# A third tile pair of the cross-attention output product as seven half-size products

## Chip, cores and metric

One core of one Trainium2 chip runs the kernel as one program. The metric is the device time of an execution in microseconds (us). Everything is float32 unless a line says otherwise.

## The reference, cut to what matters

The kernel computes one layer of a bidirectional encoder for 768 tokens (256 of a prompt, 512 of a sample) of width 1024: a mixer (self attention and convolution), a cross attention into 256 memory tokens per sequence, and a mixture of experts. Each of the three is added to 2^0.25 times its input and normalised by a LayerNorm. The change lies in the last line of the cross attention and the LayerNorm behind it:

```python
p = jax.nn.softmax(sc, axis=-1).astype(v.dtype)
o = jnp.einsum('bhqk,bkhd->bqhd', p, v).reshape(b, s, D_MODEL)
return o @ w_o                                      # 768x1024 @ 1024x1024
...
h = _layer_norm(DEEPNORM_ALPHA * h + xa, ln2_g[l], ln2_b[l])
ff = _hier_moe(h, w_router_g[l], ...)               # logits = h @ router, top-1 group, top-2 experts
```

## The kernel before, in words

The 768 rows are six tiles (0 to 5) of 128 rows; `hres` holds them by rows, `hT` and `cat` hold transposed copies. Each engine has one program of its own, in a fixed order written by hand, and semaphores join them. PSUM's eight banks are handed out ahead of time by `plan_banks` (turns of four banks for products, two for transposes); a `claim` waits until the bank's last user has read it, `full` waits until a bank is filled.

**The output product.** The weight w_o lies in two slabs of 1024x512. For a pair of tiles (a = 0: tiles 0 and 1, a = 1: tiles 2 and 3), the pair is seen as a 2x2 block matrix (A11, A12, A21, A22: two tiles by two halves of the inner dimension), the weight as 2x2 blocks too, and the product is made from seven half-size block products P1 to P7 instead of eight (`co_term`, L2340 to L2345, matmuls on L2344). VectorE makes the sums of blocks that go into them: `row_sums` (L1682 to L1688, into `scr`) for the rows, and once the sums of the weights (L1397, L1725, L1726). It then adds each product into `hres` (`term_sum`, L1692 to L1707, L1506), except that ScalarE copies P1 out first (L1206). Tiles 4 and 5 are done plainly: for each tile and each half of the columns, eight matmul steps of 512 columns (`product`, L2008), which one VectorE instruction adds to the row (`residual`, L1461).

**The LayerNorm behind it (LN_2).** For tiles 0 to 4: VectorE takes mean and variance (`dve_stats`, L744 and L746), GpSimd makes two coefficients (`pool_coef`, L718 to L720), ScalarE scales the row (`act_hat`, L736), GpSimd multiplies by the gain (`pool_gain`, L729), VectorE adds the bias (`dve_bias`, L761) and signals `ln_done`. The list `SHORT` (L537) names norms that take a shorter way, tile 5 among them: after the statistics VectorE itself does (row - mean) x gain (L754), waits for GpSimd's coefficient, and does x rstd + bias (L757). ScalarE and GpSimd's gain are left out.

**Behind the norm, on TensorE:** `h2_T(i)` transposes tile i once `ln_done` has come (L2020), ScalarE copies it to `cat` (`rows_T`, L1002), and `route(i)` multiplies it by the 36 columns of the router (L2334). The order before is: pair 0's seven products; pair 1's with h2_T(0) ahead of P4; h2_T(1); the products of tile 4 with route(0) between its halves; h2_T(2); tile 5's with route(1); h2_T(3); route(2); h2_T(4); route(3); route(4); h2_T(5); route(5). Then VectorE turns the logits into tables of rows (L1758 on), and the mixture of experts begins with GpSimd's gathers of rows from DRAM (L905).

**On the DMA queue of SyncE:** the normalised tiles are stored to `h2_rows` (L649), each after its `ln_done`. Before the store of tile 2, the queue waits for P3 of the last pair and then loads expert 0's down weights and expert 1's gate and up weights (L632, L627), over buffers that the seven products used. After the last store it waits for the last output product and loads more experts. In the expert stage weights stream all the time, each load waiting until its buffer has been used.

```python
            for i in range(NT):                                        # SyncE
                if i == 2:
                    full(sp, ("co7", CO_PAIRS - 1, TERMS[-1]))
                    load_d(0, 0)
                    load_gu(1, 1)
                sp.wait_ge(ln_done, dones(LN_2[i]))
                sp.dma_start(h2_dram[i * P:(i + 1) * P, :], hres[:, i, :]).then_inc(h2_stored, 16)
```

Of the kernel before, what the change touches and what calls it, by code (L numbers as in the profile page):

```python
# [25 lines left out]
P = 128  # L26
# [4 lines left out]
NT = T // P  # L31
# [72 lines left out]
MEAN_AT, VAR_AT = 9, 12  # L104
TERMS = ("P1", "P2", "P6", "P7", "P4", "P5", "P3")
CQ_CHUNKS = KC // 2
CO_PAIRS = 2
MIX_TERMS = [(a, term) for a in range(2) for term in TERMS[:2]] + [(a, term) for a in range(2) for term in TERMS[2:]]
CO_WEIGHTS_AT = {10: 0, 12: 1, 14: 2, 16: 3}
TH = T // 2  # L110
# [42 lines left out]
def plan_banks():  # L153

    place, used, turn = {}, [0] * 8, {}

    def take(kind, key):
        banks = {"mm": (0, 1, 2, 3), "tr": (4, 5), "pv": (6, 7), "first": (4, 5, 6, 7)}[kind]
        b = banks[turn.get(kind, 0) % len(banks)]
        turn[kind] = turn.get(kind, 0) + 1  # L160
        place[key] = (b, used[b])
        used[b] += 1

    for i in range(NT):
# [12 lines left out]
    for key in ("qT", "kT"):  # L177
        turn["tr"] += turn["tr"] % 2

    def qk(i):  # L180
        take("tr", ("qT", i))
        take("tr", ("kT", i))

    qk(0)
    qk(1)
    for k in range(STEPS + 3):
        if k < STEPS:
            take("mm", ("sS", 2 * k))
# [36 lines left out]
    for a in range(CO_PAIRS):  # L225
        for term in TERMS:
            take("mm", ("co7", a, term))
    for i in range(2 * CO_PAIRS, NT):
        for j in range(2):
            take("mm", ("co", i, j))  # L230
    for i in range(NT):
        for j in range(2):
            take("tr", ("hT", 2, i, j))
    take("pv", "route")
    for key in ("rank", "count", "counts", "order", "caps"):
        take("mm", key)
    take("tr", "firstD")
    for key in ("firstA", "firstB"):
        take("pv", key)
    for key in ("base", "list"):  # L240
        place[key] = (7, used[7])
        used[7] += 1
    return place, used


def encoder(nc, x, mem, w_slabs, lnp, ln_cols, rope_cos, rope_sin, q_gain, k_gain, cpar_dram, w_router, b_router,
# [7 lines left out]
    with ExitStack() as ctx:  # L254
# [69 lines left out]
        co3 = 3 - sum(co_at)  # L324
        coT = {"T3": ring[:, co3, 0:2048], "T2": ring[:, co3, 2048:4096], "T4": early[:, 4096:6144], "T1": early[:, 6144:8192]}
        coS = {f"S{n + 1}": scr[:, 4096 + 512 * n:4608 + 512 * n].rearrange("p (k t) -> p k t", k=4) for n in range(4)}
        coU = [memx[:, 1024 * a:1024 * a + 512] for a in range(CO_PAIRS)]
        coV = [memx[:, 1024 * a + 512:1024 * a + 1024] for a in range(CO_PAIRS)]

        def co_rows(a):  # L330

# [186 lines left out]
        slab_last = {"a": ("a", CC - 1, 1), "g": ("g", CC - 1, 1), "q": ("q", NT - 1), "kv": ("kv", NT - 1)}  # L518
        for j in range(2):
            slab_last |= {f"mix{j}": (("mx", 0, "P5"), ("mx", 1, "P3"))[j], f"ck{j}": ("ck", 4 * j + 3), f"cv{j}": ("cv", "P4", MT // 2 - 1),  # L520
                          f"cq{j}": ("cq", "P3", CQ_CHUNKS - 1), f"co{j}": ("co", NT - 1, j)}


        slab_last["cv1"] = ("cq", "P5", CQ_CHUNKS - 1)
# [11 lines left out]
        LN_2 = [LN_1[-1] + 1 + i for i in range(NT)]  # L536
        LN_3 = [LN_2[-1] + 1 + i for i in range(NT)]  # L537

        SHORT = (LN_2[-1], LN_3[-1])
        FOLD = LN_X + LN_M  # L540

        def hats(n):
# [13 lines left out]
        def _(sp):  # L556
# [86 lines left out]
            for i in range(NT):  # L643
# [3 lines left out]
                    load_gu(1, 1)  # L647
                sp.wait_ge(ln_done, dones(LN_2[i]))
                sp.dma_start(h2_dram[i * P:(i + 1) * P, :], hres[:, i, :]).then_inc(h2_stored, 16)  # L649
            full(sp, ("co", NT - 1, 1))  # L650
            load_d(1, 1)
            load_gu(3, 3)
            load_d(2, 2)
# [111 lines left out]
        def _(pool):  # L765
# [170 lines left out]
                                ALU.mult).then_inc(low_ready, 1)  # L936
            pool.wait_ge(h2_stored, 16 * NT)
            pool.wait_ge(tabs_done, 1)
            full(pool, ("co", NT - 1, 1))
            gather(0)  # L940
            gather(1)
            pool.wait_ge(tabs_done, 3)
# [46 lines left out]
        def _(act):  # L989
# [211 lines left out]
                bank = full(act, key)  # L1201
                a.activation(cq_out(0, 1, c), bank[:, 0:TH], ACT.Copy, scale=MHD ** -0.5).then_inc(free(key), 1)
            exps("x", CROSS, STEPS)
            for a2 in range(CO_PAIRS):
                bank = full(act, ("co7", a2, "P1"))
                a.activation(coU[a2], bank, ACT.Copy).then_inc(free(("co7", a2, "P1")), 1)  # L1206
            act_hat(act, LN_2[0])
            act_hat(act, LN_2[1])
            rows_T(2, 0)
            rows_T(2, 1)  # L1210
            act_hat(act, LN_2[2])
            act_hat(act, LN_2[3])
            rows_T(2, 2)
            act_hat(act, LN_2[4])
            for i in range(3, NT):
                rows_T(2, i)

            act.wait_ge(h2_stored, 16 * NT)
# [47 lines left out]
        def _(dve):  # L1266
# [411 lines left out]
            def row_sums(a, part):  # L1678

                (A11, A12), (A21, A22) = co_rows(a)  # L1680
                if part == 0:
                    v.tensor_tensor(coS["S1"], A21, A22, ALU.add).then_inc(co_combined, 1)  # L1682
                    dve.wait_ge(co_combined, 5 + 6 * a)
                    v.tensor_tensor(coS["S2"], coS["S1"], A11, ALU.subtract).then_inc(co_combined, 1)
                    return
                v.tensor_tensor(coS["S3"], A11, A21, ALU.subtract).then_inc(co_combined, 1)
                dve.wait_ge(co_combined, 6 + 6 * a)
                v.tensor_tensor(coS["S4"], A12, coS["S2"], ALU.subtract).then_inc(co_combined, 1)  # L1688

            def add_term(a, term, i, j):  # L1690
# [49 lines left out]
            term_sum(1, "P5")  # L1740
            dve_stats(dve, LN_2[2], link)
            term_sum(1, "P3")
            dve_stats(dve, LN_2[3], link)
            for k in range(2 * CO_PAIRS, NT):
                for j in range(2):
                    residual(("co", k, j), k, j).then_inc(free(("co", k, j)), 1)
                    if k == 4:
                        dve_bias(dve, LN_2[2 + j], link)
                    was_read(dve, ("co", k, j))
                dve_stats(dve, LN_2[k], link)  # L1750
                if k == 4:
                    dve_bias(dve, LN_2[4], link)
            dve_bias(dve, LN_2[-1], link)


# [232 lines left out]
        def _(pe):  # L1988
# [333 lines left out]
                for c in range(CQ_CHUNKS):  # L2322
                    was_read(pe, ("cq", term, c))
            attention("x", CROSS, len(SELF))
            wo = [slab("co0"), slab("co1")]
            for j in range(2):
                was_read(pe, ("xO", CROSS[-1][0], j))

# [22 lines left out]
            for a in range(CO_PAIRS):  # L2351
                (A11, A12), (A21, A22) = co_rows(a)
                co_term(a, "P1", A11, coB[0][0])
                co_term(a, "P2", A12, coB[1][0])
                pe.wait_ge(co_combined, 6 + 6 * a)
                co_term(a, "P6", coS["S2"], coT["T2"])
                pe.wait_ge(co_combined, 7 + 6 * a)
                co_term(a, "P7", coS["S3"], coT["T3"])
                if a == 0:
                    pe.wait_ge(co_combined, 9)  # L2360
                else:
                    h2_T(0)
                co_term(a, "P4", A22, coT["T4"])
                if a == 0:
                    pe.wait_ge(co_combined, 10)
                co_term(a, "P5", coS["S1"], coT["T1"])
                pe.wait_ge(co_combined, 8 + 6 * a)
                co_term(a, "P3", coS["S4"], coB[1][1])
            h2_T(1)
            for i in range(2 * CO_PAIRS, NT):  # L2370
                for j in range(2):
                    last = product(("co", i, j), lambda k: k, lambda k: hTv[:, k, i * P:(i + 1) * P],
                                   lambda k: wo[j][:, k, :])
                    done(("co", i, j), last)
                    if j == 0:
                        route(i - 4)
                h2_T(i - 2)
            route(2)
            h2_T(NT - 2)
            route(3)  # L2380
# [215 lines left out]
```

## Time and profile before

| | us |
|---|---|
| runs: median (lowest to highest), 3 runs | 1031.46 (1028.77 to 1032.88) |
| the profiled execution's own time | 1032.55 |
| its span, first to last instruction | 1030.8 |
| TensorE matmul busy in the span | 912.4 |
| VectorE / ScalarE / GpSimd busy | 528.8 / 237.0 / 316.4 |
| mean granted TensorE clock, as a share of 2.4 GHz | 0.952 |

Times in a profile count from the start of the span. A row of a timeline merges instructions of one kind that follow each other; "x16" counts records, and two records are one matmul step here. What stands in brackets behind a row is the idle time of the engine ahead of it and who ended it.

### The profile page before, as it was taken

What the parts mean: (1) busy time and instruction counts of PE and PEld (TensorE: products, weight loads), DVE (VectorE), ACT (ScalarE), POOL (GpSimd) and SP (SyncE); (2) the same over time, 40 slices, a digit from 0 to 9 for tenths busy, and PEclk for the clock granted to TensorE, in tenths of its full rate; (3) what the DMA queues carried; (4) which work ended last, traced back from release to release, by engine and by line L of the source; (5) the groups of instructions that cost most, each with busy time, mean ns of one, the idle gap of its engine ahead of it and who ended that gap; (6) DMA issues with size and microseconds to landing.
All of it is one profiled execution on the core that took longest, in us unless ns stands there. A gap on an engine that the chain in (4) does not pass through costs nothing.

```text
span 1030.8 us, 10108 instructions
## 1 busy us (share of the span) xinstructions
PE 912.4 (89%) x3322; PEld 471.9 (46%) x3322; DVE 528.8 (51%) x830; ACT 237.0 (23%) x582; POOL 316.4 (31%) x352
## 2 busy tenths in 40 slices
PE   4999999799989899999999999958969999999900
PEld 4555466344444444445567544553434444444300
DVE  4999999964532189837235564364311111211156
ACT  5321423334483111201004301131101111111101
POOL 6921042434453242400004404213241221112047
PEclk9999999899999999999999999967989999999955
DMA  9310301403003002220041123275997999998562
GB/s 344 130 42 0 123 0 37 127 1 82 1 1 123 1 0 82 82 82 1 0 147 58 63 101 126 99 294 191 420 400 296 417 421 419 387 410 352 178 251 118
DMA packets 46198, 165.11 MB, mean 160 GB/s; under 512 B 8641, under 2 KB 14145, under 8 KB 33857
## 3 DMA queue, kind: packets, MB, share of 16 engines
q1 hardware_dynamic: 39424, 151.85, 38.1%
q0 software_dynamic: 6720, 12.60, 3.3%
q8 instruction: 28, 0.46, 0.2%
q14 instruction: 26, 0.20, 0.1%
HBM read 156.88 MB, written 18.03 MB: 170 GB/s over the span
## 4 chain that ended last, share of the span: by engine, by line
PE 55%; DVE 4%; POOL 4%; issue 3%; DMA 2%; ACT 1%; POOLq 0%; DVEq 0%
PE ps L2474 8%; PE ps L2503 7%; PE ps L2305 7%; PE ps L2477 5%; PE ps L2344 5%; PE ps L2278 5%; PE ps L2240 3%; PE ps L2008 3%; PE ps L2186 2%; PE ps L2451 2%; PE ps L2111 2%; PE ps L2083 2%; POOL hres L729 2%; PE ps L2334 1%; PE ps L2020 1%
## 5 line engine op out<-in xcount | busy, mean ns | idle before, releaser
L1324 DVE SCALAR_TENSOR_TENSOR cat<-early,cpar,cat 128x798 f32<-128x798 f32 (+2 forms) x150 | 143.7, 958 | 4.9
L844 POOL TENSOR_SCALAR hT<-hT,rinv 128x512 f32<-128x512 f32 (+1 forms) x48 | 67.8, 1424 | 93.3 <-DVE rinv L1446 93.3
L2008 PE MATMUL ps<-ring,hT 128*128 128x512 f32 (+1 forms) x256 | 91.9, 520 | 0.0
L2008 PE MATMUL ps<-hT,ring 128*128 128x256 f32 (+1 forms) x256 | 84.8, 494 | 4.2 <-issue 2.5
L910 POOL DMA_INDIRECT pair_rows<-hT,sidx x22 | 22.0, 1002 | 181.7 <-DVE hT L1935 180.8
L1925 DVE COPY memx<-ps 128x256 f32<-128x256 f32 x22 | 9.3, 424 | 131.2 <-PE ps L2486 131.2
L2008 PEld LDWEIGHTS ps<-ring,hT 128*128 128x128 f32 x256 | 49.0, 193 | 39.7 <-issue 37.3
L2008 PEld LDWEIGHTS ps<-hT,ring 128*128 128x128 f32 x256 | 49.7, 195 | 38.1 <-issue 32.5
L718 POOL TENSOR_SCALAR lnt<-mv 128x1 f32<-128x1 f32 x28 | 14.2, 507 | 162.2 <-DVE mv L746 161.1
L1438 DVE TENSOR_REDUCE nmax<-ps 128x2 f32<-128x1024 f32 (+1 forms) x24 | 25.1, 1046 | 74.1 <-PE ps L2136 74.0
L851 POOL TENSOR_SCALAR memx<-memx,rinv 128x256 f32<-128x256 f32 x24 | 22.0, 924 | 129.7 <-DVE rinv L1402 129.7
L2503 PE MATMUL ps<-ring,memx 128*64 128x512 f32 (+1 forms) x144 | 58.7, 601 | 0.7 <-DVE memx L1925 0.7
L1935 DVE COPY hT<-ps 128x512 f32<-128x512 f32 x22 | 15.2, 692 | 65.8 <-PE ps L2503 65.8
L2474 PE MATMUL ps<-early,hT 128*64 128x512 f32 x128 | 44.8, 636 | 0.8 <-ACT hT L1230 0.8
L1130 ACT ACTIVATE hT<-ps,nmax 128x512 f32<-128x512 f32 (+1 forms) x48 | 29.1, 611 | 69.5 <-DVE nmax L1438 69.4
L736 ACT ACTIVATE hres<-hres,lnc 128x1024 f32<-128x1024 f32 x22 | 27.2, 1239 | 70.0 <-POOL lnc L720 70.0
L2477 PE MATMUL ps<-early,hT 128*128 128x512 f32 x96 | 42.5, 596 | 0.0
L2474 PE MATMUL ps<-ring,hT 128*64 128x512 f32 x96 | 42.3, 594 | 0.0
L2305 PE MATMUL ps<-hT,ring 128*128 128x384 f32 x128 | 41.6, 486 | 0.0
L1237 ACT ACTIVATE memx<-ps 128x256 f32<-128x256 f32 x22 | 8.4, 383 | 142.9 <-PE ps L2474 79.3
L2186 PE MATMUL ps<-ring,cat 128*128 128x512 f32 x64 | 31.2, 634 | 6.4 <-DVE hres L1461 4.5
L1655 DVE SCALAR_TENSOR_TENSOR cat<-ps,cat 128x384 f32<-128x384 f32 x28 | 15.2, 556 | 41.2 <-PE ps L2305 41.2
(337 smaller groups left out, 1759.6 us busy)
## 6 DMA issues: line engine op xcount, KB each, us to landing
ring<-w_down SPq DMA_DIRECT2D x16, 1024.0 KB, 17.2
early<-w_gate SPq DMA_DIRECT2D x12, 1024.0 KB, 9.6
early<-w_up SPq DMA_DIRECT2D x12, 1024.0 KB, 13.7
ring<-w_gate SPq DMA_DIRECT2D x10, 1024.0 KB, 12.9
ring<-w_up SPq DMA_DIRECT2D x10, 1024.0 KB, 16.0
scr<-w_down SPq DMA_DIRECT2D x8, 1024.0 KB, 15.7
cat<-w_down SPq DMA_DIRECT2D x8, 1024.0 KB, 15.5
scr<-w_gate SPq DMA_DIRECT2D x5, 1024.0 KB, 9.2
```

Of the source, the lines that this page charges most:

```text
L844: g.tensor_scalar(sprob[u % 4][:, 0:width], sprob[u % 4][:, 0:width], rinv[:, u % 4:u % 4 + 1], None, ALU.mult).then_inc(prob_ready, 1)
L1130: a.activation(sprob[u % 4][:, 0:width], ps[:, place[key][0], 0:width], ACT.Exp, bias=nmax[:, u % 4:u % 4 + 1], accum_out=rsum[:, u % 4:u ...
L1324: ins = v.scalar_tensor_tensor(out=out, in0=src, scalar=cpar[:, c, k:k + 1], in1=out, op0=ALU.mult, op1=ALU.add)
L2008: last = t.matmul(out_of(bank), lhs(k), rhs(k), start=(k == 0), stop=(k == KC - 1))
L2186: last = t.matmul(bank, catv[:, k, i * P:(i + 1) * P], w[:, k, :], start=(k == 0), stop=(k == KC - 1))
L2240: last = t.matmul(bank, rows[:, k, :], wk[:, k, :], start=(k == 0), stop=(k == 3))
L2278: last = t.matmul(bank, rows[:, k, i * P:(i + 1) * P], wk[:, k, :], start=(k == 0), stop=(k == 3))
L2305: last = t.matmul(bank[:, 0:TH], wk[:, k, c * P:(c + 1) * P], rows[:, k, :], start=(k == 0), stop=(k == 3))
L2344: last = t.matmul(bank, rows[:, k, :], wk[:, k, :], start=(k == 0), stop=(k == 3))
L2474: last = t.matmul(gu_out(64 * h, 64 * h + 64, b), xT[b][:, k, 64 * h:64 * h + 64], gu_of(n % GU_SLOTS, k), start=(k == 0), stop=(k == KC - 1))
L2477: last = t.matmul(gu_out(0, P, b), xT[b][:, k, :], gu_of(EXPERT_BLOCKS[j][1] % GU_SLOTS, k), start=(k == 0), stop=(k == KC - 1))
L2503: last = t.matmul(ps[h0:h1, 2 + n, :], hidT[b][:, k, h0:h1], w[:, k, n * 512:(n + 1) * 512], start=(k == 0), stop=(k == 1))
```

## The change

A third pair (tiles 4 and 5) goes the way of the seven products, so nothing is left for the plain product here. TensorE's order for it is P1, P2, P6, P7, h2_T(2), P4, route(0), route(1), P5, P3, h2_T(3); then, as before, route(2), h2_T(4), route(3), route(4), h2_T(5), route(5). The short norm is used for tile 4 too. The waits on "the last output product" now name P3 of the third pair; that is so on SyncE's queue too, ahead of the two early expert loads. The temporaries of pair 2 are those of pair 0, and ScalarE's copy of its P1 stands ahead of its scaling of tiles 2 and 3.

```diff
-CO_PAIRS = 2
+CO_PAIRS = 3
+CO_ROWS = (4, 10, 14)
...
-        coU = [memx[:, 1024 * a:1024 * a + 512] for a in range(CO_PAIRS)]
+        coU = [memx[:, 1024 * (a % 2):1024 * (a % 2) + 512] for a in range(CO_PAIRS)]
...
-        SHORT = (LN_2[-1], LN_3[-1])
+        SHORT = (LN_2[-2], LN_2[-1], LN_3[-1])
...
-            full(sp, ("co", NT - 1, 1))
+            full(sp, ("co7", CO_PAIRS - 1, "P3"))
...
+            first_term(0)
+            first_term(1)
             act_hat(act, LN_2[0])
             act_hat(act, LN_2[1])
             rows_T(2, 0)
             rows_T(2, 1)
+            first_term(2)
             act_hat(act, LN_2[2])
             act_hat(act, LN_2[3])
-            rows_T(2, 2)
-            act_hat(act, LN_2[4])
-            for i in range(3, NT):
+            for i in range(2, NT):
                 rows_T(2, i)
...
             term_sum(1, "P3")
+            row_sums(2, 0)
             dve_stats(dve, LN_2[3], link)
-            for k in range(2 * CO_PAIRS, NT):
-                for j in range(2):
-                    residual(("co", k, j), k, j).then_inc(free(("co", k, j)), 1)
-                    if k == 4:
-                        dve_bias(dve, LN_2[2 + j], link)
-                    was_read(dve, ("co", k, j))
-                dve_stats(dve, LN_2[k], link)
-                if k == 4:
-                    dve_bias(dve, LN_2[4], link)
+            row_sums(2, 1)
+            term_sum(2, "P2")
+            dve_bias(dve, LN_2[2], link)
+            term_sum(2, "P6")
+            term_sum(2, "P7")
+            dve_bias(dve, LN_2[3], link)
+            term_sum(2, "P4")
+            term_sum(2, "P5")
+            dve_stats(dve, LN_2[4], link)
+            term_sum(2, "P3")
+            dve_stats(dve, LN_2[5], link)
+            dve_bias(dve, LN_2[4], link)
             dve_bias(dve, LN_2[-1], link)
...
                 if a == 0:
                     pe.wait_ge(co_combined, 9)
                 else:
-                    h2_T(0)
+                    h2_T(2 * a - 2)
                 co_term(a, "P4", A22, coT["T4"])
                 if a == 0:
                     pe.wait_ge(co_combined, 10)
+                elif a == 2:
+                    route(0)
+                    route(1)
                 co_term(a, "P5", coS["S1"], coT["T1"])
-                pe.wait_ge(co_combined, 8 + 6 * a)
+                pe.wait_ge(co_combined, CO_ROWS[a] + 4)
                 co_term(a, "P3", coS["S4"], coB[1][1])
-            h2_T(1)
-            for i in range(2 * CO_PAIRS, NT):
-                for j in range(2):
-                    last = product(("co", i, j), lambda k: k, lambda k: hTv[:, k, i * P:(i + 1) * P],
-                                   lambda k: wo[j][:, k, :])
-                    done(("co", i, j), last)
-                    if j == 0:
-                        route(i - 4)
-                h2_T(i - 2)
+                if a >= 1:
+                    h2_T(2 * a - 1)
             route(2)
             h2_T(NT - 2)
```

## Rows read from the trace of the kernel before

**Rows 1.** Busy engines by stretch (PE, PEld, DVE, ACT, POOL), granted clock, DMA share, GB/s.
```profile
588.30:638.20 49.90, 49.87 (x128) 23.05 (x129) 30.79 (x43) 4.86 (x7) 8.95 (x11) 1.00 0.27 106
638.20:670.10 31.90, 31.90 (x106) 16.56 (x105) 10.15 (x13) 5.56 (x7) 9.23 (x10) 1.00 0.37 148
```

**Rows 2.** Chain that ended last, around the routing products: start, us, what.
```profile
673.79 3.50 PE ps L2334 x32
...
682.73 0.40 DVE ring L1758
```

**Rows 3.** TensorE's longest wait between 704.8 and 978.2 us: total, times, longest.
```profile
PE ps L2451 <- DMA hT<-h_rows,gidx: 8.3, 1, 8.3
```

**Rows 4.** TensorE's timeline: start, us, line, tiles, records, idle before.
```profile
638.22 7.03 PE L2008 MATMUL ps<-ring,hT 128*128 128x512 f32 x16
645.09 1.87 PE L2334 MATMUL ps<-wr,cat 128*128 128x36 f32 x16
...
670.14 1.04 PE L2020 MATMUL ps<-ident,hres 128*128 128x128 f32 x8
...
672.72 1.07 PE L2020 MATMUL ps<-ident,hres 128*128 128x128 f32 x8
...
677.12 1.07 PE L2020 MATMUL ps<-ident,hres 128*128 128x128 f32 x8
679.02 3.60 PE L2334 MATMUL ps<-wr,cat 128*128 128x36 f32 x16 [0.83 <-ACT cat L1002]
```

**Rows 5.** VectorE's timeline: the end of pair 0, then the short norm of tile 5.
```profile
610.53 1.29 DVE L744 BATCH_NORM_STATS2 stats<-hres 128x6 f32<-128x512 f32 x2
611.85 0.21 DVE L746 BATCH_NORM_AGGREGATE mv<-stats 128x2 f32<-128x12 f32 x1
612.64 0.69 DVE L1692 TENSOR_TENSOR hres<-hres,ps 128x512 f32<-128x512 f32 x1 [0.58 <-PE ps L2344]
...
672.70 1.29 DVE L754 SCALAR_TENSOR_TENSOR hres<-hres,mv,gb 128x1024 f32<-128x1024 f32 x1
675.20 1.28 DVE L757 SCALAR_TENSOR_TENSOR hres<-hres,lnc,gb 128x1024 f32<-128x1024 f32 x1 [1.21 <-POOL lnc L720]
```

**Rows 6.** GpSimd's timeline: the first of the three coefficient steps of tile 5.
```profile
672.75 1.31 POOL L718 TENSOR_SCALAR lnt<-mv 128x1 f32<-128x1 f32 x1 [10.38 <-DVE mv L746]
```

**Rows 7.** Busy engines by stretch, columns as in rows 1.
```profile
676.00:678.00 2.00, 2.00 (x20) 1.95 (x19) 0.48 (x1) 0.21 (x1) 0.00 (x0) 1.00 0.36 143
...
679.10:682.60 3.50, 3.50 (x16) 3.37 (x16) 0.00 (x0) 3.04 (x4) 0.00 (x0) 0.50 0.94 365
...
310.50:313.70 3.20, 3.20 (x5) 1.18 (x4) 0.00 (x0) 1.97 (x6) 0.00 (x0) 0.50 0.97 314
...
324.00:328.00 4.00, 2.27 (x9) 1.11 (x8) 1.95 (x4) 1.93 (x5) 3.10 (x2) 1.00 0.01 2
```

**Rows 8.** TensorE's timeline: two earlier waits, and transposes at the lower clock.
```profile
309.29 5.40 PE L2186 MATMUL ps<-ring,cat 128*128 128x512 f32 x8 [1.96 <-ACT cat L1177]
...
326.09 3.67 PE L2186 MATMUL ps<-ring,cat 128*128 128x512 f32 x8 [1.73 <-DVE hres L1461]
...
702.00 1.95 PE L2451 MATMUL ps<-ident,hT 128*128 128x128 f32 x8
```

**Rows 9.** The last early expert load: its issue on SyncE's queue, and its landing (last column, us).
```profile
683.50 0.43 SPq L627 DMA_DIRECT2D cat<-w_up  x1
...
cat<-w_up SPq DMA_DIRECT2D x1, 1024.0 KB, 14.0
```

**Rows 10.** GpSimd's first gather, landing of first and of all (median), and the DMA rate.
```profile
696.61 3.12 POOL L905 DMA_INDIRECT hT<-h_rows,gidx  x1 [0.94 <-POOL gidx L888]
...
hT<-h_rows,gidx POOLq DMA_INDIRECT x1, 5.3
...
hT<-h_rows,gidx POOLq DMA_INDIRECT x22, 9.8
...
685.00:690.00 5.00, 1.18 (x18) 1.00 (x18) 4.52 (x19) 0.67 (x3) 0.81 (x1) 0.50 1.02 429
```

More of the change, by code:

```diff
@@ L227, in plan_banks @@
             take("mm", ("co7", a, term))
-    for i in range(2 * CO_PAIRS, NT):
-        for j in range(2):
-            take("mm", ("co", i, j))
     for i in range(NT):
@@ L326, in encoder @@
         coS = {f"S{n + 1}": scr[:, 4096 + 512 * n:4608 + 512 * n].rearrange("p (k t) -> p k t", k=4) for n in range(4)}
-        coU = [memx[:, 1024 * a:1024 * a + 512] for a in range(CO_PAIRS)]
-        coV = [memx[:, 1024 * a + 512:1024 * a + 1024] for a in range(CO_PAIRS)]
+        coU = [memx[:, 1024 * (a % 2):1024 * (a % 2) + 512] for a in range(CO_PAIRS)]
+        coV = [memx[:, 1024 * (a % 2) + 512:1024 * (a % 2) + 1024] for a in range(CO_PAIRS)]
         def co_rows(a):
@@ L520, in encoder @@
             slab_last |= {f"mix{j}": (("mx", 0, "P5"), ("mx", 1, "P3"))[j], f"ck{j}": ("ck", 4 * j + 3), f"cv{j}": ("cv", "P4", MT // 2 - 1),
-                          f"cq{j}": ("cq", "P3", CQ_CHUNKS - 1), f"co{j}": ("co", NT - 1, j)}
+                          f"cq{j}": ("cq", "P3", CQ_CHUNKS - 1), f"co{j}": ("co7", CO_PAIRS - 1, "P3")}
         slab_last["cv1"] = ("cq", "P5", CQ_CHUNKS - 1)
@@ L938, in _ @@
             pool.wait_ge(tabs_done, 1)
-            full(pool, ("co", NT - 1, 1))
+            full(pool, ("co7", CO_PAIRS - 1, "P3"))
             gather(0)
@@ L1203, in _, with first_term @@
             exps("x", CROSS, STEPS)
-            for a2 in range(CO_PAIRS):
+            def first_term(a2):
                 bank = full(act, ("co7", a2, "P1"))
+                if a2 >= 2:
+                    act.wait_ge(co_combined, 6 * a2)
                 a.activation(coU[a2], bank, ACT.Copy).then_inc(free(("co7", a2, "P1")), 1)
+            first_term(0)
+            first_term(1)
             act_hat(act, LN_2[0])
@@ L1682, in row_sums @@
                     v.tensor_tensor(coS["S1"], A21, A22, ALU.add).then_inc(co_combined, 1)
-                    dve.wait_ge(co_combined, 5 + 6 * a)
+                    dve.wait_ge(co_combined, CO_ROWS[a] + 1)
                     v.tensor_tensor(coS["S2"], coS["S1"], A11, ALU.subtract).then_inc(co_combined, 1)
@@ L1686, in row_sums @@
                 v.tensor_tensor(coS["S3"], A11, A21, ALU.subtract).then_inc(co_combined, 1)
-                dve.wait_ge(co_combined, 6 + 6 * a)
+                dve.wait_ge(co_combined, CO_ROWS[a] + 2)
                 v.tensor_tensor(coS["S4"], A12, coS["S2"], ALU.subtract).then_inc(co_combined, 1)
@@ L2324, in _ @@
             attention("x", CROSS, len(SELF))
-            wo = [slab("co0"), slab("co1")]
+            slab("co0")
+            slab("co1")
             for j in range(2):
@@ L2354, in _ @@
                 co_term(a, "P2", A12, coB[1][0])
-                pe.wait_ge(co_combined, 6 + 6 * a)
+                pe.wait_ge(co_combined, CO_ROWS[a] + 2)
                 co_term(a, "P6", coS["S2"], coT["T2"])
-                pe.wait_ge(co_combined, 7 + 6 * a)
+                pe.wait_ge(co_combined, CO_ROWS[a] + 3)
                 co_term(a, "P7", coS["S3"], coT["T3"])
@@ L2365, in _ @@
                     pe.wait_ge(co_combined, 10)
+                elif a == 2:
+                    route(0)
+                    route(1)
                 co_term(a, "P5", coS["S1"], coT["T1"])
-                pe.wait_ge(co_combined, 8 + 6 * a)
+                pe.wait_ge(co_combined, CO_ROWS[a] + 4)
                 co_term(a, "P3", coS["S4"], coB[1][1])
-            h2_T(1)
-            for i in range(2 * CO_PAIRS, NT):
-                for j in range(2):
-                    last = product(("co", i, j), lambda k: k, lambda k: hTv[:, k, i * P:(i + 1) * P],
-                                   lambda k: wo[j][:, k, :])
-                    done(("co", i, j), last)
-                    if j == 0:
-                        route(i - 4)
-                h2_T(i - 2)
+                if a >= 1:
+                    h2_T(2 * a - 1)
             route(2)
```

## The prediction

> **What bounds the kernel now.** I read the busy time by stretch first. From the first of the seven products to the last plain product TensorE is busy without a gap at the full clock, 49.87 of 49.90 us and 31.90 of 31.90 us, while VectorE does 10.15 us of work in the second stretch [rows 1]. So a matmul step taken away there shortens the stretch, as long as nothing behind it comes late. The chain of waits says the same for what follows: it runs over the routing products and ends them in VectorE's logits at 682.73 us, behind route(5) [rows 2]. From there on everything hangs on that moment: VectorE's tables, the first gather, the expert blocks. In the expert stage TensorE's one long wait is 8.3 us for a gather [rows 3], and that gather stands in GpSimd's own order behind earlier blocks, so it moves along with the start. A microsecond won or lost before 682.73 us is therefore a microsecond of the whole, to a first approximation. The question is only when route(5) ends.
>
> **The products.** Sixteen records, eight steps of 512 columns, take 645.09 - 638.22 = 6.87 us [rows 4], 0.429 us a record. The plain way for two tiles is 4 x 16 = 64 records, 27.5 us. The seven products are 7 x 8 = 56 records of the same shape, 24.05 us. That is 3.43 us less. Transposes and routes are as many as before. h2_T(3), which began at 670.14 us, now begins at 666.7 us.
>
> **VectorE** gets more: four residual adds go, and four row sums and eleven adds come, each like the 0.69 us add [rows 5], so 11 x 0.69 = 7.6 us more, and the short norm of tile 4 is 1.29 + 1.28 us in place of one bias add. With 10.15 us busy of 31.90 [rows 1] it has room: about 19 us of work in 28.5. The sums that P6 needs are made while P1 and P2 run: VectorE has P3 of pair 1 at some 637.6 us, then one add, two row sums, statistics and two more row sums, 0.69 x 5 + 1.5 = 5 us, so done at 642.6, and P6 starts at 645.1. Cost nothing; if that cover went, each late microsecond would be one of TensorE's.
>
> **ScalarE and GpSimd.** ScalarE must now take out P1 of pair 2 (ready at 641.8 us) before it scales tiles 2 and 3. Tile 2's norm then ends near 647.5 us and h2_T(2) wants it at 652; tile 3's ends near 655.5 and h2_T(3) wants it at 666.7. Nothing again. Tile 4's scaling and gain disappear from both engines.
>
> **The tail** is where the gain goes. Before, tile 4 was complete one whole tile of matmuls ahead of its transposes. Now tiles 4 and 5 are both complete only near the end: tile 4 with P5, tile 5 with P3, and both norms follow one another on VectorE. It sees P3 0.2 us after the product's last step, at 666.9 us; then, from [rows 5], the add with its gap 0.72, statistics of tile 5 1.32 + 0.25, L754 of tile 4 1.33, L757 of tile 4 1.28: done(4) is 671.8 us. The statistics of tile 5 stand ahead of both steps of tile 4 in the order, so nothing shortens this. TensorE has done h2_T(3) (0.87) and route(2) (1.70) by 669.3 and **waits 2.6 us**, with routes 3 to 5 and h2_T(5) queued behind the waiting h2_T(4). That starts at 671.9 instead of 672.72 us [rows 4]: 0.8 us of the 3.43 are left. Tile 5's norm is no second wait: L754 until 673.1, and L757, held up at most by GpSimd's coefficients (a step of them lasted 1.31 us beside VectorE's L754 [rows 6]), until 674.8 at the latest; h2_T(5) can't come before 671.9 + 0.9 + 3.5 = 676.3.
>
> **The clock** prices that wait. In 676 to 678 us it was granted in full (2.4 GHz); after that came h2_T(5), 0.83 us of waiting, and route(5) ran at 0.50 (1.2 GHz) for its whole length [rows 4, 7]: 3.60 us, against 1.87 for the same sixteen records earlier. Stretches of small work with a short wait thus lose the clock here, and the cold route did not win it back. A 1.96 us wait between transposes and products was followed by 0.50 too, a 1.73 us wait elsewhere was not [rows 7, 8]. The new wait of 2.6 us lies between a route and transposes, so I take it that the clock falls in it or just behind it, some 7 us sooner than before. What then runs cold and ran warm before: h2_T(4) and h2_T(5), 1.95 against 1.07 us each [rows 4, 8], and route(3) and route(4), 3.60 against 1.87. Together 2 x 0.88 + 2 x 1.73 = 5.2 us. Less the 0.8 us, route(5) ends 4.4 us later; where the clock falls only behind h2_T(4) and a little into route(3), 3.2 us. The other end of this unknown cost is zero. I take the cold end, because the nearest rows (route(5) itself, 0.83 us of waiting) show the fall. Other executions of the kernel before may have lost the clock a little ahead of 679 us, which makes their routes dearer, so I take 3.5 us, low in that span.
>
> The Trainium skill (TensorE: Matmul & The Clock Gate, section "Why this matters for your kernels") speaks of longer idle gaps than this one as what costs the clock. By it the wait would be harmless and the sum 0.8 us faster. The rows of 0.83 and 1.96 us of waiting speak against it, that of 1.73 us for it.
>
> **The DMA queue.** SyncE's wait for "P3 of the last pair" now ends at 666.9 us, not at about 637.5. Behind it stand the down weights of expert 0, gate and up of expert 1, and the stores of tiles 2 and 3, all 29 us or so later; then the stores of tiles 4 and 5 and all other early loads. From 666.9 us these are ten loads of 1.05 MB and four stores of 0.52 MB, 12.6 MB, at the 429 GB/s of a full queue [rows 10] 29.4 us: with 2 us until data flows, all is in at 698.3 us. Before, the last of them landed at 683.50 + 14.0 = 697.5 us [rows 9], and the first gather went out at 696.61 [rows 10]. With route(5) 3.5 us later the gather goes out near 700.1, so the queue is empty. The stores are in by about 681 us and are wanted only by that gather and by ScalarE's scaling, which had some 15 us of slack. Cost nothing; without the later route(5) the first gather would be the one hit.
>
> **Sum** against the profiled execution's own 1032.55 us (span 1030.8, 1.75 around it): -3.43 for the products, +2.6 for the wait, about +4.3 for the clock, so +3.5, 1036.05. That execution lies 1.1 us above the median of the runs, 1031.46, so the median should become **1035.0 us**.
>
> **Rivals.** (a) The clock holds as before: 0.8 us faster, and if the early loads and the gather meet for a microsecond, nothing: about 1030.6 us. For it: the 1.73 us row. (b) The wait doesn't come, because VectorE reaches tile 4's norm sooner than I add up: the full 3.4 us, 1028.0. Against it: each of its five steps has a row. (c) Slower by more than 0.5%: the cold clock, and the first gather behind weights that now come late. A gather in a full queue lands in 9.8 us (median of all), the first took 5.3 [rows 10]: 4.5 us on the path, 1039.5. It decides once the queue is filled past the gather's issue, 2 us more than I reckon; the later route(5), which itself holds back the last three loads, can do that. (d) That the change doesn't do what it says: 56 records in place of 64 are plain in the code, so next to no chance.
>
> **How the numbers follow.** Forecast 0.63, with 1033.4 to 1036.8 as its own range (3.2 to 4.4 us and the spread of the medians, about 1 us); (a) 0.20, (b) 0.04, (c) 0.13. A measurement of this kernel can tell about 0.5%, 5.2 us: slower means above 1036.6, faster below 1026.3. Most of (c) and a small part of the forecast's cases lie above: 0.17. Below lies almost nothing, 0.02; the rest 0.81. Range 1029.8 to 1038.2: it takes in most of (a) and the near part of (c), and leaves out (b) and the far part of (c).
>
> **What would show it.** Right: 56 records between 638.2 and 666.5 us without a gap; a wait of about 2.6 us ahead of tile 4's transposes, ended by VectorE's L757; the clock at 0.50 from there; routes 3 and 4 together near 7 us; VectorE's first logit step near 686 us; tiles 2 and 3 stored, and two experts' weights loaded, from 667 us on. Wrong: no such wait (the adding up of VectorE's order fails); the wait there but the routes at 1.7 us (the clock step fails, and (a) holds); a gap ahead of P6 of pair 2 (the cover by P1 and P2 fails); a first gather of far over 5 us (c).

## The result, and the profile after

The changed kernel took 1037.91 us in the median of six runs (1035.71 to 1039.97); a seventh, slow one at a mean granted clock of 0.818 took 1154.83 us and is left out. The kernel before took 1032.88 us in the median of seven. The ratio is 1.0050, with a 95% interval of 1.0029 to 1.0072: slower by half a per cent. Twelve more executions later (e12 below) gave 1035.52 against 1031.91 us, 1.0047 (1.0031 to 1.0063). The profiled execution took 1035.75 us, its span is 1034.0.

First, TensorE's timeline of the changed kernel from the double route on (start, us, line, tiles, records, idle before). It answers to [rows 4].

```profile
658.17 3.66 PE L2342 MATMUL ps<-wr,cat 128*128 128x36 f32 x32
661.66 3.68 PE L2352 MATMUL ps<-early,scr 128*128 128x512 f32 x8
665.17 3.60 PE L2352 MATMUL ps<-ring,scr 128*128 128x512 f32 x8
668.61 1.04 PE L2027 MATMUL ps<-ident,hres 128*128 128x128 f32 x8
669.48 1.87 PE L2342 MATMUL ps<-wr,cat 128*128 128x36 f32 x16
673.83 1.97 PE L2027 MATMUL ps<-ident,hres 128*128 128x128 f32 x8 [2.47 <-DVE hres L755]
675.59 6.88 PE L2342 MATMUL ps<-wr,cat 128*128 128x36 f32 x32
682.28 1.95 PE L2027 MATMUL ps<-ident,hres 128*128 128x128 f32 x8
685.00 3.60 PE L2342 MATMUL ps<-wr,cat 128*128 128x36 f32 x16 [0.78 <-ACT cat L1000]
```

The times are to be read from the start of the seven products, since the stages ahead of them, which the change doesn't touch, took 1.90 us longer in this execution (first product at 590.23, before 588.33). So h2_T(3) starts at 78.4 us, before at 81.8: the 3.43 us are there, to the hundredth. Then comes the wait, 2.47 us ahead of tile 4's transposes, and everything behind it takes nearly twice as long: transposes 1.97 us for eight records, not 1.07; thirty-two records of routes 6.88, not 3.66. The clock is in the next rows (stretch, busy PE, PEld, DVE, ACT, POOL, granted clock, DMA share, GB/s), which answer to [rows 1, 7]: full with no gap ahead of the wait, and half of 2.4 GHz behind it. The row with 0.85 is the one in which it falls: TensorE's last route ended at 671.35 us, so the clock fell inside the wait, and not in the small work ahead of it. VectorE has 14.65 us of work in the first stretch, more than before and still only half of it.

```profile
638.20:666.90 28.70, 28.70 (x104) 15.49 (x103) 14.65 (x23) 5.14 (x7) 7.97 (x8) 1.00 0.00 1
...
671.00:672.00 1.00, 0.35 (x4) 0.24 (x3) 0.96 (x2) 0.00 (x0) 0.79 (x1) 1.00 0.99 418
672.00:673.00 1.00, 0.00 (x0) 0.00 (x0) 0.96 (x2) 0.00 (x0) 0.92 (x2) 0.85 1.03 434
...
674.10:682.20 8.10, 8.10 (x40) 8.10 (x40) 2.15 (x2) 1.19 (x2) 0.89 (x2) 0.50 0.98 361
```

Who makes TensorE wait is seen on VectorE, which answers to [rows 5]:

```profile
668.02 0.21 DVE L744 BATCH_NORM_AGGREGATE mv<-stats 128x2 f32<-128x12 f32 x1
668.88 0.69 DVE L1695 TENSOR_TENSOR hres<-hres,ps 128x512 f32<-128x512 f32 x1 [0.65 <-PE ps L2352]
669.60 1.29 DVE L742 BATCH_NORM_STATS2 stats<-hres 128x6 f32<-128x512 f32 x2
...
671.17 1.28 DVE L752 SCALAR_TENSOR_TENSOR hres<-hres,mv,gb 128x1024 f32<-128x1024 f32 x1
672.49 1.28 DVE L755 SCALAR_TENSOR_TENSOR hres<-hres,lnc,gb 128x1024 f32<-128x1024 f32 x1
673.69 1.28 DVE L752 SCALAR_TENSOR_TENSOR hres<-hres,mv,gb 128x1024 f32<-128x1024 f32 x1
675.20 1.29 DVE L755 SCALAR_TENSOR_TENSOR hres<-hres,lnc,gb 128x1024 f32<-128x1024 f32 x1 [0.23 <-POOL lnc L718]
688.71 0.38 DVE L1765 TENSOR_TENSOR ring<-ps,br 128x216 f32<-128x216 f32 x1 [12.22 <-PE ps L2342]
```

Tile 4's statistics are ready at 668.23, but its two norm steps (L752, L755) stand behind the add of P3 and tile 5's statistics and end at 673.77. The first logit step comes at 688.71, that is 98.48 us from the first product; before it was 682.73, 94.40. The stage is 4.08 us longer. It divides at the start of tile 4's transposes: they begin 0.79 us sooner than before (83.60 against 84.39 us from the first product), and from there to the logit step it is 14.88 us in place of 10.01, 4.87 more.

The queue of early loads on SyncE, answering to [rows 9], and the landings of its last load and of the first gather (last column, us):

```profile
668.80 0.33 SPq L630 DMA_DIRECT2D scr<-w_down  x1
...
676.88 0.54 SPq L630 DMA_DIRECT2D ring<-w_down  x1
...
689.48 0.43 SPq L625 DMA_DIRECT2D cat<-w_up  x1
```

```profile
cat<-w_up SPq DMA_DIRECT2D x1, 1024.0 KB, 13.8
hT<-h_rows,gidx POOLq DMA_INDIRECT x1, 5.4
```

The loads do come 29 us later, and the first gather still lands in 5.4 us (5.3 before). From the logit step to the first expert product it is 22.1 us in both kernels. Behind that the two differ in one place, the first expert product itself: before and after,

```profile
704.78 9.54 PE L2474 MATMUL ps<-early,hT 128*64 128x512 f32 x32 [0.83 <-ACT hT L1230]
```

```profile
710.85 7.09 PE L2478 MATMUL ps<-early,hT 128*64 128x512 f32 x32 [0.83 <-ACT hT L1233]
```

Before, the block began at half the clock, which came back 5 us later; here it was back just ahead of the block (0.79 in the mean of 709 to 712 us). That is 2.45 us in favour of this one execution. The span's account: 1.90 us more ahead of the products, 4.08 + 0.09 more to the first expert product, 2.45 less in the expert block that it begins, 0.4 less in small differences behind, 3.2 more in all.

### The profile page after: what moved, and what is told of

Its sections match the earlier page's. It is cut to its first block, busy times and chain, and to the rows that moved or that the text cites. A ratio compares the mean times of both kernels' runs of the same rounds, so it can differ in the third digit from the quotient of the medians.

```text
span 1034.0 us, 10106 instructions
## 1 busy us (share of the span) xinstructions
PE 913.7 (88%) x3314; PEld 474.7 (46%) x3314; DVE 535.9 (52%) x842; ACT 236.5 (23%) x582; POOL 316.3 (31%) x351
## 4 chain that ended last, share of the span: by engine, by line
PE 55%; DVE 4%; POOL 4%; issue 3%; DMA 2%; ACT 1%; POOLq 0%; SPq 0%; DVEq 0%
PE ps L2478 8%; PE ps L2507 7%; PE ps L2352 7%; PE ps L2312 7%; PE ps L2481 5%; PE ps L2285 5%; PE ps L2247 3%; PE ps L2193 2%; PE ps L2455 2%; PE ps L2118 2%; PE ps L2090 2%; POOL hres L727 2%; PE ps L2342 1%; PE ps L2027 1%; DMA hT<-h_rows,gidx 1%
## 5 line engine op out<-in xcount | busy, mean ns | idle before, releaser
L2015 PE MATMUL ps<-ring,hT 128*128 128x512 f32 (+1 forms) x192 | 63.8, 495 | 0.0
L2015 PEld LDWEIGHTS ps<-ring,hT 128*128 128x128 f32 x192 | 37.0, 193 | 26.5 <-issue 24.1
L2478 PE MATMUL ps<-early,hT 128*64 128x512 f32 x128 | 42.4, 594 | 0.8 <-ACT hT L1233 0.8
```

The costliest lines, as they stand in the source:

```text
L2015: last = t.matmul(out_of(bank), lhs(k), rhs(k), start=(k == 0), stop=(k == KC - 1))
L2478: last = t.matmul(gu_out(64 * h, 64 * h + 64, b), xT[b][:, k, 64 * h:64 * h + 64], gu_of(n % GU_SLOTS, k), start=(k == 0), stop=(k == KC - 1))
```

## The experiments

Two measures are used. The stage: from the first of the seven products to VectorE's first logit step (before 94.40 us, changed 98.48) and to the first expert product (116.45 and 120.62). And the ratio to the kernel before over twelve executions or so, with its interval. The stage is free of what the clock does elsewhere in an execution, the ratio isn't. But each stage is read from a single profiled execution. How well it repeats is seen in the changed kernel: 98.48, 98.50 (e6, where only later loads are moved) and 98.47 us (e12). "Warm" and "cold" mean the full and the half granted clock; `warm(n)` in a diff is n unused matmul steps of 512 columns.

### e1: no wait, but more small work on end

```diff
                 elif a == 2:
-                    route(0)
-                    route(1)
...
+            route(0)
+            route(1)
             route(2)
             h2_T(NT - 2)
```

> The changed kernel with route(0) and route(1) moved behind P3 and h2_T(3), so that they fill the wait ahead of tile 4's transposes. Measure: from the first of the seven products to VectorE's first logit step (before 94.4 us, changed kernel 98.5 us). Theory W (the wait of 2.5 us costs the clock): no wait is left, the clock stays full until about the last wait, 91 us, the whole kernel some 3.4 us faster than before. Rival S (a long stretch of small work alone costs the clock, wait or not; here it is 3.4 us longer): the clock falls on the way, 94 to 96.5 us, and the whole is 0 to 2 us slower than before.

Measured: 96.1 us to the logit step; ratio 1.0017 (1.0002 to 1.0033). TensorE's timeline, and the clock:

```profile
663.16 1.04 PE L2027 MATMUL ps<-ident,hres 128*128 128x128 f32 x8
664.04 5.78 PE L2342 MATMUL ps<-wr,cat 128*128 128x36 f32 x48
669.62 1.95 PE L2027 MATMUL ps<-ident,hres 128*128 128x128 f32 x8
```

```profile
664.00:667.00 3.00, 3.00 (x30) 3.00 (x28) 2.90 (x5) 0.89 (x2) 1.34 (x2) 1.00 0.81 295
...
669.00:669.60 0.60, 0.60 (x5) 0.60 (x5) 0.52 (x1) 0.00 (x0) 0.60 (x1) 0.50 1.03 437
...
669.70:680.00 10.30, 10.30 (x49) 9.89 (x48) 1.29 (x1) 1.79 (x3) 0.00 (x0) 0.50 1.01 368
```

The wait is gone: no idle time stands in front of the transposes. The clock fell nevertheless, at the end of three routes on end, with TensorE busy all the time. Theory W as I had it, that only waiting costs the clock, falls; S gave the stage and the ratio. S isn't a rule for how long small work may go on, though: here the clock fell 5.8 us behind the last product (at 669.0 us), while the kernel before kept it for 8.9 us, with 0.83 us of waiting at their end [rows 4, 7]. The stage is 2.35 us shorter than the changed kernel's, nearly the whole wait.

### e5: the wait alone, in the kernel before

```diff
             route(2)
+            pe.wait_ge(ln_done, dones(LN_2[-1]))
             h2_T(NT - 2)
```

> The kernel before, with one wait added: h2_T(4) waits for tile 5's norm. The products are untouched, and so is the small work; only a wait of about 3.8 us is put in. Theory W: 3.8 us of waiting and the clock falls with it, 5.2 us more, 103 us to the first logit step. Rival (the clock depends on the small work alone, which is here as before): it falls where it did, 98.2 us.

```profile
676.37 1.97 PE L2020 MATMUL ps<-ident,hres 128*128 128x128 f32 x8 [3.65 <-DVE hres L757]
678.13 6.88 PE L2334 MATMUL ps<-wr,cat 128*128 128x36 f32 x32
```

Measured: 103.1 us, as Theory W said; one execution of 1041.31. A wait of 3.65 us costs 8.7. The small work is the same as before and the clock fell all the same 3.5 us sooner, in the wait. So waiting costs the clock too. What e1 and e5 have in common is that TensorE goes without 512-column work; that this lack is the cause is my reading, not something that one run isolates. h2_T(4) began 3.8 us later than before; the rest, 8.7 - 3.8 = 4.9 us, is the price of the cold tail and nearly the 5.2 us of the prediction.

### e2: the wait filled with unused full matmul steps

```diff
             route(2)
+            warm(3)      # t.matmul(<free bank>, hTv[:, 0, 0:P], hTv[:, 1, 0:512]) x3, result unused
             h2_T(NT - 2)
```

> The changed kernel with three more matmul steps of 512 columns (2.6 us of work, result unused) between route(2) and h2_T(4), in the time of the wait. Theory W and rival S both: the clock stays full through h2_T(4) and route(3), and falls at the earliest in route(4); 93.5 to 95 us to the first logit step, the whole within 1 us of before. If the transposes and routes stay at 1.95 and 3.4 us all the same, the clock isn't what made the tail slow, and both fall.

```profile
668.77 2.82 PE L2385 MATMUL ps<-hT 128*128 128x512 f32 x6
671.43 1.09 PE L2027 MATMUL ps<-ident,hres 128*128 128x128 f32 x8
...
677.76 1.95 PE L2342 MATMUL ps<-wr,cat 128*128 128x36 f32 x16 [0.83 <-ACT cat L1000]
...
701.41 1.97 PE L2461 MATMUL ps<-ident,hT 128*128 128x128 f32 x8 [2.13 <-DMA hT<-h_rows,gidx]
```

Measured: 92.0 us to the logit step, better than expected, since route(5) too was warm (1.95 us, not 3.60). Tile 4's transposes begin at 83.61 us from the first product, as in the changed kernel (83.60), and the small work behind them is the same; only the clock differs, full from 671.5 to 679.5 us here. So the clock alone is 6.5 us of the changed kernel's stage. That is the direct proof of the price; 4.9 us of it are new, the rest, route(5), was paid in the kernel before as well. But the first expert product came at 116.40 us, as before, because TensorE now waits 2.13 us for the first gather, which landed in 7.7 us:

```profile
hT<-h_rows,gidx POOLq DMA_INDIRECT x1, 7.7
```

The ratio is 1.0007 (0.9988 to 1.0025): no difference to the kernel before.

### e3: tile 4's norm ahead of P3's add

```diff
+            dve_bias(dve, LN_2[4], link)
             term_sum(2, "P3")
             dve_stats(dve, LN_2[5], link)
-            dve_bias(dve, LN_2[4], link)
```

> The changed kernel with both steps of tile 4's short norm on VectorE ahead of the add of P3 and the statistics of tile 5. done(4) comes 1.9 us sooner, so the wait ahead of h2_T(4) shrinks from 2.5 to about 0.6 us; tile 5's norm now ends some 1.5 us later and h2_T(5) may wait up to 1 us. Theory W: the clock holds through routes 3 and 4, 93 to 94.5 us to the first logit step, whole about 1 us faster than before. Rival S: the clock falls as in the changed kernel, some 97 us.

```profile
672.40 1.45 PE L2027 MATMUL ps<-ident,hres 128*128 128x128 f32 x8 [0.74 <-DVE hres L755]
673.64 6.88 PE L2342 MATMUL ps<-wr,cat 128*128 128x36 f32 x32
```

Measured: 96.2 us, ratio 1.0022 (1.0003 to 1.0040). The wait shrank to 0.74 us, as reckoned, and the clock fell in the transposes all the same (1.45 us, between 1.07 and 1.95). W's holding clock again fails, and the 96.2 us are near S's 97. The clock fell 0.6 us behind the end of this short wait (at 673.0 us), so a part played by the wait isn't excluded here; e1 is the clean case.

### e4: the long norm for tile 4

```diff
-        SHORT = (LN_2[-2], LN_2[-1], LN_3[-1])
+        SHORT = (LN_2[-1], LN_3[-1])
...
-            for i in range(2, NT):
+            rows_T(2, 2)
+            act_hat(act, LN_2[4])
+            for i in range(3, NT):
                 rows_T(2, i)
```

> The changed kernel with the long norm (ScalarE, GpSimd, VectorE) for tile 4, as before. done(4) then comes through GpSimd's gain, 2.35 us, and a bias add: about 0.7 us later than by the short way, so the wait ahead of h2_T(4) is 3.2 us and the first logit step at 99.2 us. If the short norm is what makes tile 4 late, it comes sooner instead, below 98.5.

Measured: 99.4 us (one execution), the wait 3.37 us instead of 2.47. The short norm is right for tile 4 and worth 0.9 us; it isn't the cause.

### e6 and e7: the last three early loads held back

```diff
-            load_d(3, 3)
-            load_gu(4, 4)
             sp.wait_ge(scratch_done, 1)
+            load_d(3, 3)
+            load_gu(4, 4)
```

> The changed kernel with the loads of expert 3's down weights and expert 4's gate and up weights held back until VectorE's tables are made, so that the DMA queue is empty sooner. Theory (the clock alone made the changed kernel slow, its first gather isn't hit by the late loads): 98.5 us to the first logit step and 120.6 us to the first expert product, as in the changed kernel. Rival Q (the crowded queue costs too): the first expert product comes 1 us or more sooner than 120.6.

Measured, in the changed kernel (e6, one execution): 98.50 and 120.59 us, no change. The crowded queue cost the changed kernel nothing: its first gather goes out at 702.60 us, and from 702 to 703 us the DMA share there is 0.06, so its late route(5) had let the queue all but drain.

> The changed kernel with the three filling matmul steps and the held-back loads together. With the fill alone the first logit step came at 92.0 us, but the first expert product at 116.4 (before: 94.4 and 116.45), with TensorE 2.1 us waiting for the first gather. Theory Q (that wait is the price of the early loads coming 29 us late): it goes, first expert product at 114.3 us, the whole 2 to 2.5 us faster than before. Rival (the first gather takes this long for another reason): 116.4 us, no gain.

Measured, in e2's kernel (e7): 93.65 us to the logit step and 115.79 to the first expert product, so 22.1 us between the two in place of e2's 24.4, and no wait for the gather, which landed in 5.4 us. Theory Q is right in its mechanism: the early loads that come 29 us later cost 2.3 us as soon as the tail is fast. But the logit step came 1.7 us later than in e2, and that is the second find. TensorE between P4 and P5:

```profile
657.02 4.07 PE L2342 MATMUL ps<-wr,cat 128*128 128x36 f32 x32
660.90 4.97 PE L2352 MATMUL ps<-early,scr 128*128 128x512 f32 x8
```

```profile
657.10:660.00 2.90, 2.90 (x29) 2.90 (x27) 0.69 (x1) 0.00 (x0) 0.00 (x0) 1.00 0.00 0
661.00:664.30 3.30, 3.30 (x6) 1.43 (x6) 0.00 (x0) 0.00 (x0) 0.00 (x0) 0.62 0.00 0
```

The two routes that the change put together lost the clock in this execution, without any wait, and P5 took 4.97 us in place of 3.68. Seven other profiles have the same order up to there (the changed kernel's two, e2, e3, e4, e6, e8), and all of them kept the clock through it. So the first expert product came at 115.79 and not at the 114.3 of Theory Q. Ratio 0.9987 (0.9969 to 1.0005); the 2 to 2.5 us expected of the whole aren't shown.

### e8 and e9: unused steps in the stretch up to the experts

```diff
             h2_T(NT - 1)
+            warm(1)
             done("route", route(NT - 1))
+            warm(6)
...
+            warm(3)
             first(0)
```

> The kernel with the fill and the held-back loads, and more unused matmul steps of 512 columns: one ahead of route(5), six behind it, three ahead of the first table product, all in time in which TensorE waits for others. Theory (the cold clock is the price of the stretch between the products and the expert stage): transposes of the first gathered rows at 1.07 us in place of 1.95, the first expert block in 7 us in place of 9.2; the whole 5 to 6 us faster than before. Rival (the clock falls all the same in the 9 us that stay unfilled ahead of the first block): as the kernel with fill and held-back loads.

> The kernel before, with the held-back loads and the same unused steps (one ahead of route(5), six behind it, three ahead of the first table product; none in the wait ahead of h2_T(4), which it hasn't). It tells what is the fill's and what the third pair's: if the clock holds here too, the gain over before is 3 to 5 us, and the third pair with the same fill is ahead of it by 0.8 us (3.43 less 2.6 of wait), no more.

Measured: e8 91.99 and 113.88 us, ratio 0.9988 (0.9968 to 1.0007); e9 (kernel before, held-back loads, same steps) 92.74 and 114.63 us, ratio 1.0002 (0.9983 to 1.0020). Both held the clock through route(5), but not up to the first block (it fell at 696.5 and 694.5 us); e8's transposes of the gathered rows are cold:

```profile
701.23 1.97 PE L2464 MATMUL ps<-ident,hT 128*128 128x128 f32 x8
```

In e8's profile the clock was back just ahead of the first expert block, which took 7.09 us, the 7 expected; e9's took 9.14. But the changed kernel's profile had 7.09 without any such step, so this is no proof for them. The expected 5 to 6 us (e8) and 3 to 5 us (e9) did not come: e8 won 2.6 us in the stage, e9 1.8, and neither interval excludes 1. One number was met: with the clock equal in both up to the logit step, the third pair is 92.74 - 91.99 = 0.75 us ahead, the forecast's 3.43 - 2.6 = 0.8.

### e10: the two routes apart, beside the changed kernel again (e12)

```diff
                 elif a == 2:
                     route(0)
-                    route(1)
                 co_term(a, "P5", coS["S1"], coT["T1"])
+                if a == 2:
+                    route(1)
```

> The changed kernel with route(1) moved from between P4 and P5 (right behind route(0)) to between P5 and P3. In the kernel with fill and held-back loads the clock fell in that double route without any wait, and P5 was 1.4 us longer. Theory D (3.4 us of routes on end can cost the clock in some executions, which is why those of the changed kernel lie in two groups, about 1035.7 and 1039.1): the upper group goes, median 1 to 3 us below the changed kernel's in the same runs. Rival: the two groups have another cause, the median stays within 0.7 us of it. The one profile shows no difference behind P3 in either case, 98.5 us to the first logit step.

> The changed kernel, unaltered, in the runs of the two kernels beside it. By both theories 3 to 7 us slower than before; it is there for its median and for whether its executions lie in two groups again.

Measured: e10 median 1035.32 us, ratio 1.0032 (1.0016 to 1.0048); e12 1035.52, 1.0047 (1.0031 to 1.0063). e10's stage is 98.50 us, the 98.5 expected. The median hardly moved, against Theory D. But of e12's twelve executions four lie at 1038.3 to 1039.5 us, as three of the first six did at 1039.0 to 1040.0, and of e10's ten none lies above 1036.9. That would fit the double route as the upper group's cause. One profile is of that group, and it speaks against it: e12's profiled execution took 1038.34 us, and its double route, P5 and first expert block are:

```profile
658.43 3.66 PE L2342 MATMUL ps<-wr,cat 128*128 128x36 f32 x32
661.92 3.68 PE L2352 MATMUL ps<-early,scr 128*128 128x512 f32 x8
...
711.11 8.65 PE L2478 MATMUL ps<-early,hT 128*64 128x512 f32 x32 [0.83 <-ACT hT L1233]
```

The double route and P5 are as long as in the execution of 1035.75 us, and so is the stage (98.47 and 120.61 us). Of the 2.6 us between the two spans 0.27 lie ahead of the products, 1.56 in the first expert block, where the clock came back only at 714.3 us, and 0.8 behind it. So this execution's place in the upper group has nothing to do with the double route; what put the others there isn't known.

### e11: put together

```diff
                 elif a == 2:
                     route(0)
-                    route(1)
+                    h2_T(3)
                 co_term(a, "P5", coS["S1"], coT["T1"])
+                if a == 2:
+                    route(1)
...
             route(2)
+            route(3)
             h2_T(NT - 2)
-            route(3)
+            warm(1)
             route(4)
             h2_T(NT - 1)
+            warm(1)
             done("route", route(NT - 1))
+            warm(6)
```

(with e3's order of the norm, e8's three steps ahead of the first table product, and e6's loads)

> What the runs point to, put together: seven products for all tiles; tile 4's norm ahead of tile 5's statistics; each small piece between full products (P4, route(0), h2_T(3), P5, route(1), P3); route(2) and route(3) in the time of the wait; one unused step in each of the two waits for ScalarE's copies, six behind route(5), three ahead of the first table product; the last three early loads held back. Theory: no wait over 1 us ahead of h2_T(4), the clock full up to route(5), the first logit step at 90 us (before 94.4), the whole 4 to 6 us faster than before. Rival (nearly 8 us of small work on end with two single steps in it still lose the clock): 92 to 94 us, 1 to 3 us faster.

```profile
669.48 3.84 PE L2342 MATMUL ps<-wr,cat 128*128 128x36 f32 x32
673.12 1.95 PE L2027 MATMUL ps<-ident,hres 128*128 128x128 f32 x8
674.87 1.70 PE L2387 MATMUL ps<-hT 128*128 128x512 f32 x2
676.40 1.87 PE L2342 MATMUL ps<-wr,cat 128*128 128x36 f32 x16
```

Measured: 91.8 us to the logit step and 113.7 to the first expert product, median 1028.46 against 1031.91 us, ratio 0.9971 (0.9957 to 0.9985): faster than the kernel before by 0.3%, and than the changed one by 0.7% (1028.46 against e12's 1035.52). No wait is left ahead of tile 4's transposes. The clock fell in routes 2 and 3 even so (the transposes take 1.95 us) and was back for route(4). The 3.45 us between the medians and the 91.8 us both lie just beyond the rival's 1 to 3 us and 92 to 94, and short of the theory's. What the new order adds to e8 isn't shown: the stages differ by 0.2 us (91.8 and 92.0), and the intervals of the two ratios overlap.

## Why the prediction was right, point by point

- **Products.** 3.43 us less, and 3.43 measured (81.8 against 78.4 us for h2_T(3)). No wait for a sum of blocks, and tiles 2 and 3 were never late: right.
- **The wait.** 2.6 us forecast, 2.47 measured, ended by VectorE's second norm step for tile 4 (L755, the L757 of before) as said; tile 4's transposes begin 0.79 us sooner than before, the forecast's 0.8. Tile 5's norm was held up by GpSimd's coefficients, 0.23 us, and no one waited for it: right. One reckoning beside it was off: about 19 us of VectorE work in the 28.5 us of the products. Some 14.6 us lie there; the rest of the 19 is the tail itself, from P3's add to tile 4's norm.
- **The clock.** It fell in the wait, at 672.7 us, and for the transposes and routes named, at the prices named (1.97, 6.88, 1.95). Forecast 3.2 to 4.4 us later at route(5)'s end, measured 4.08; I took 3.5. The clock's own term is 4.87 us, where the sum had about 4.3 and the full reckoning 5.2. The size was right, and so was "the clock falls in the wait" for this order; as an account of what costs the clock it is only half, for in e1 it falls without a wait. What fits all the runs is time without 512-column work, of which waiting is one part and routes and transposes the other. It is no measure: from the end of the last full product to the fall it was 4.1 us here, 3.1 in e7, 5.8 in e1 and 8.9 in the kernel before. The rows of before hinted at it: route(5) had run cold behind a wait of only 0.83 us, which I read as the fault of the wait.
- **The rule on idle gaps.** By the Trainium skill (TensorE: Matmul & The Clock Gate, "Why this matters for your kernels") the gap here is shorter than the ones it warns of, so by that rule alone the clock should have held. It fell in the gap of 2.47 us, and in e1 it fell with no gap at all; the measurement decides.
- **What the sum left out.** route(0) and route(1) on end between P4 and P5. I priced the move at nothing, since the number of routes is the same. In e7's profile it cost 1.3 us in P5 and 0.4 in the routes, in the seven other profiles with this order nothing, e12's among them. So that is a risk left out; it isn't the reason for e12's 1038.34 us, and for the other executions near 1039 us nothing shows it.
- **The time of the whole, and luck in it.** The first six executions gave 1037.91 us, 2.9 above the 1035.0 forecast and 0.3 inside the range; the twelve of e12 gave 1035.52. The ratios, 1.0050 and 1.0047, are the better test, since the 1035.0 stood on three runs of the kernel before; the forecast's was 1.0034. That the profiled execution took 1035.75 us, with 1036.05 in the sum, is luck: the 1.90 us ahead of the products and the 2.45 us back in the first expert block, neither of which the prediction had, nearly cancel. Both vary by themselves: over the fourteen profiles the first product starts at 587.08 to 590.54 us, and the first expert block takes 7.09 to 9.73 us.
- **The DMA queue.** "Cost nothing" was right for the changed kernel (e6), and so was the remark that only the late route(5) hides it: e2 paid 2.1 us, e7 got it back. The reckoning under it was off: the last three loads wait for route(5), so the last landing was 703.3 us (689.48 + 13.8), 0.7 us behind the gather's issue, and not at 698.3 with the queue empty by then. The 2 us until data flows stood on no row; here it flows about 0.8 us after the first load's issue at 668.80.
- **Rivals.** (a), the clock holds, is what e2 made by force: 2.4 us faster in the stage, not 0.8, as route(5) got warm too, and then given back to the gather. (b) did not come, and (c)'s mechanism didn't either: the first gather landed in 5.4 us. The ratio of 1.0050 lies at (c)'s bound all the same, by the clock alone as far as the stage tells.

## What to carry to other kernels

Before taking dense matmuls away from a stage, look at what small work (transposes, narrow matmuls) and which waits are left in a row behind or between them: the clock may fall there, and small work costs nearly twice as much at half the clock (3.60 against 1.87 us). Here 3.4 us of matmuls were saved, 2.6 went into a new wait and 4.9 to the clock. A wait filled with unused full steps gave the 6.5 us back (e2). Keeping small pieces apart, each between full products, is worth a try, though no run here shows its gain alone. Finish the rows that are needed first before starting on the statistics of the next, and when the tail gets faster, look at which loads were so far out of its way.

## What the runs showed of the hardware that I had not expected

- The clock fell under a TensorE that was never idle: three routes of 36 columns on end, 5.6 us (e1), and once even two of them (e7, at 660.1 us, 3.1 us into them), after which a product had a mean granted clock of 0.62 over 3.3 us. Seven profiles of the same order kept the clock through the same two routes, so this differs from one execution to the next.
- The stretch without 512-column work ahead of a fall lasted from some 3 us (e7, e9) to 9.7 us (e2, behind its unused steps). The same small work kept the clock in one execution and lost it in the next.
- A single unused step of 512 columns behind cold transposes, 1.70 us, stood between them and a warm route in e11: the clock was back within it. Whether the step brought it back, no run here tells.
- GpSimd's three coefficient steps on 128x1 took from 671.22 to 675.10 us while VectorE ran its row steps back to back; the same three took 1.2 us for tile 4, with VectorE idle or reading PSUM.
